# The weights' high and low parts in SBUF: slots 8200 bytes apart instead of 8192

## What is computed

```python
# block 1, per layer
x = x + 0.5 * swiglu_ffn(rmsnorm(x, ffn1_norm), ffn1_w_up, ffn1_w_down)     # d_ff 2816
x = x + mixer(rmsnorm(x, mix_norm), w_in, ...)   # q, k, v of 1536 columns, gated unit 2048, gates 2048;
                                                 # dilated attention, 31-tap convolution, projections
x = x + 0.5 * swiglu_ffn(rmsnorm(x, ffn2_norm), ffn2_w_up, ffn2_w_down)
x = rmsnorm(x, final_norm)
# block 2, per layer
p = rmsnorm_2(x, norm1) @ w_in                   # Fourier part, q, k, v
x = x + concat(norm(fourier_mix(u)), norm(windowed_gqa(q, k, v))) @ w_o
up = dwconv_centred(rmsnorm_2(x, norm2) @ w_up)  # 3 taps
x = x + (silu(gate) * val) @ w_down
```

## Time and profile before

| | |
|---|---|
| median of 3 runs | 1957.04 us (1954.49 to 1960.55) |
| profiled execution | 1957.0 us, the span as well |
| TensorE, matmuls | busy 1910.4 us (98%), 15828 |
| TensorE, weight loads | busy 1841.5 us (94%), 15828 |
| VectorE | busy 1471.9 us (75%) |
| ScalarE | busy 1104.8 us (56%) |
| GpSimd | busy 41.9 us (2%) |
| DMA | 368.57 MB, mean 188 GB/s |
| granted TensorE clock | mean 0.998 |

### The profile page before, as it was taken

How to read it: one execution, slowest core, us unless ns; L and a number is a source line. 1 busy time by engine, 2 the same in 40 slices (tenths; PEclk the granted TensorE clock), 3 DMA queues, 4 the chain that set the end, 5 groups by cost and what they waited for, 6 DMA issues and landing times.

```text
span 1957.0 us, 38879 instructions
## 1 busy us (share of the span) xinstructions
PE 1910.4 (98%) x15828; PEld 1841.5 (94%) x15828; DVE 1471.9 (75%) x2159; ACT 1104.8 (56%) x1414; POOL 41.9 (2%) x52
## 2 busy tenths in 40 slices
PE   7999999999999999999999999999999999999998
PEld 7999898799999999998988999999889999889998
DVE  6555799987765585558999877555888777878777
ACT  5444666576644464446666765444665655656554
POOL 0000011000000000000110000000000000000000
PEclk9999999999999999999999999999999999999999
DMA  6556599634555545555996446555335554435554
GB/s 251 202 178 224 190 290 272 185 99 148 208 201 185 192 172 196 183 214 183 292 279 173 107 141 217 202 184 184 130 109 196 208 193 156 141 119 192 193 193 153
DMA packets 62731, 368.57 MB, mean 188 GB/s; under 512 B 8096, under 2 KB 8352, under 8 KB 25888
## 3 DMA queue, kind: packets, MB, share of 16 engines
q1 hardware_dynamic: 54704, 339.37, 49.7%
q0 software_dynamic: 6912, 25.17, 7.2%
q10 hardware_dynamic: 1008, 2.51, 0.3%
HBM read 359.68 MB, written 1.05 MB: 184 GB/s over the span
## 4 chain that ended last, share of the span: by engine, by line
PE 74%; DVE 17%; ACT 4%; DMA 3%; issue 2%; SPq 0%; DVEq 0%; ACTq 0%
PE bank L447 23%; PE bank L448 23%; PE bank L449 22%; DVE lo L1651 5%; DVE cv L1899 4%; ACT hi L1070 1%; DVE zt L1862 1%; DMA zt<-zt 1%; DMA lo<-in_w 1%; PE bank L626 1%; PE bank L653 1%; ACT n_hi L1132 1%; PE bank L639 1%; PE bank L611 1%; DVE qk L1864 0%
## 5 line engine op out<-in xcount | busy, mean ns | idle before, releaser
L1651 DVE TENSOR_TENSOR lo<-raw,hi 128x2048 fp32r<-128x2048 f32 (+1 forms) x336 | 663.5, 1976 | 200.8 <-ACT hi L1070 200.1
L1070 ACT ACTIVATE hi<-raw 128x2048 fp32r<-128x2048 f32 (+1 forms) x336 | 598.7, 1784 | 108.8 <-PE bank L449 98.0
L447 PE MATMUL bank<-n_hi,hi 128*128 128x256 f32 x2256 | 637.9, 283 | 20.8 <-DVE lo L1926 11.5
L448 PE MATMUL bank<-n_lo,hi 128*128 128x256 f32 x2256 | 631.4, 280 | 0.0
L449 PE MATMUL bank<-n_hi,lo 128*128 128x256 f32 x2256 | 631.3, 280 | 0.0
L447 PEld LDWEIGHTS bank<-n_hi,hi 128*128 128x128 f32 x2256 | 430.8, 191 | 26.7 <-DVE lo L1926 11.5
L448 PEld LDWEIGHTS bank<-n_lo,hi 128*128 128x128 f32 x2256 | 424.9, 188 | 1.3 <-issue 1.0
L449 PEld LDWEIGHTS bank<-n_hi,lo 128*128 128x128 f32 x2256 | 425.1, 188 | 0.0
L447 PE MATMUL bank<-h_hi,hi 128*128 128x256 f32 x1152 | 330.8, 287 | 7.0 <-DVE h_lo L1655 3.9
L449 PE MATMUL bank<-h_hi,lo 128*128 128x256 f32 x1152 | 321.5, 279 | 0.0
L448 PE MATMUL bank<-h_lo,hi 128*128 128x256 f32 x1152 | 321.5, 279 | 0.0
(11 more groups left out here) (263 smaller groups left out, 2317.8 us busy)
## 6 DMA issues: line engine op xcount, KB each, us to landing
raw<-in_w SPq DMA_DIRECT2D x286, 1024.0 KB, 4.9
raw<-in_w SPq DMA_DIRECT2D x53, 512.0 KB, 4.0
lo<-in_w POOLq DMA_DIRECT2D x48, 512.0 KB, 9.1
zt<-zt SPq DMA_DIRECT2D x96, 64.0 KB, 6.9
bv<-in_bv SPq DMA_DIRECT2D x2, 768.0 KB, 6.1
spread<-in_spread SPq DMA_DIRECT2D x2, 768.0 KB, 7.9
x<-in_x ACTq DMA_DIRECT2D x4, 256.0 KB, 10.2
out_x<-sq SPq DMA_DIRECT2D x1, 1024.0 KB, 3.9
```

The lines of the kernel that those rows point to most:

```text
L447: mm(out, w_hi, a_hi, start=start, stop=False, skip_group_check=True)
L448: mm(out, w_hi, a_lo, start=False, stop=False, skip_group_check=True)
L1070: fn(hi[:, s, 0:w], raw[:, s, 0:w], ACT.Copy).then_inc(sem["hi"], 1)
L1651: v.tensor_tensor(lo[:, s, 0:w], raw[:, s, 0:w], hi[:, s, 0:w].bitcast(F32), ALU.subtract)\
```

## The change

`hi` and `lo` get 2050 elements a slot instead of 2048, of which the last two stay unused. Slot 1 so begins 8200 bytes after slot 0 and slot 2 16400 after it. Behind `hi` stand 448 further bytes, and behind `lo` 128 in the place of 192. Slot 0 of `hi` stays where it was; slot 0 of `lo` and everything behind it move up by 512 bytes and keep their place modulo 512. Modulo 512 a tile of weights begins at 128 in slot 0, 136 in slot 1 and 144 in slot 2. `raw` is not changed. The two lines that took a whole slot (1282, 1944) now name its 2048 elements. In the changed kernel a line behind 252 has a number larger by one.

```diff
--- before.py
+++ after.py
@@ -248,9 +248,10 @@
         return nc.alloc_sbuf_tensor_at(name, shape, dt, offset=at)
 
     raw = sb("raw", [P, SLOTS, CW], F32)
-    hi = sb("hi", [P, SLOTS, CW], F32R)
-    lo = sb("lo", [P, SLOTS, CW], F32R)
-    state["at"] += 192
+    hi = sb("hi", [P, SLOTS, CW + 2], F32R)
+    state["at"] += 448
+    lo = sb("lo", [P, SLOTS, CW + 2], F32R)
+    state["at"] += 128
     x = sb("x", [P, KT, S], F32)
     h_hi = sb("h_hi", [P, KT, S], F32R)
     h_lo = sb("h_lo", [P, KT, S], F32R)
@@ -1279,7 +1280,7 @@
             direct_high(2, x, gain)
             direct_high(3, x, gain)
             act.wait_ge(load[1], 16)
-            fn(hi[:, 1, :], raw[:, 1, :], ACT.Copy).then_inc(sem["hi"], 1)
+            fn(hi[:, 1, 0:CW], raw[:, 1, :], ACT.Copy).then_inc(sem["hi"], 1)
             for p in range(4):
                 fn(xsq[:, 2 * p:2 * p + 2, :], x[:, 2 * p:2 * p + 2, :], ACT.Square).then_inc(sem["sq"], 1)
             take("prm")
@@ -1941,7 +1942,7 @@
             arrived(2)
             arrived(3)
             v.wait_ge(sem["hi"], 2)
-            v.tensor_tensor(lo[:, 1, :], raw[:, 1, :], hi[:, 1, :].bitcast(F32), ALU.subtract).then_inc(sem["lo"], 1)
+            v.tensor_tensor(lo[:, 1, 0:CW], raw[:, 1, :], hi[:, 1, 0:CW].bitcast(F32), ALU.subtract).then_inc(sem["lo"], 1)
             v.wait_ge(sem["prmld"], 16)
             v.wait_ge(sem["h"], 4)
             v.tensor_copy(prm[:, 0:NP1], prm_all[:, 0:NP1]).then_inc(sem["prm"], 1)
```

## The result

The changed kernel takes **1974.75 us** in the median of 5 runs (1972.92 to 1981.69); the kernel before beside it 1957.04 us (5 runs, 1951.53 to 1966.55). The ratio is 1.0093, with a 95% interval of 1.0069 to 1.0118: slower by about 18 us, where 8.5 us less were forecast. The profiled execution has a span of 1975.5 us, and its time is 1977.33 us; so 1.8 us lie around the span, which the text ahead of the prediction took for nothing. Span against span the difference is 18.4 us.

What follows compares the result with a forecast made beforehand. The prediction took TensorE's pitch, steady at 117.6 or 113.1 ns for the same matmul, to bound the kernel. It summed 1957.0 - 10.5 (pitch drawn anew) + 2.0 (settling) = 1948.5 us, with a range of 1930 to 1974 us.

Steps and rivals of the forecast that it cites:

- What bounds the kernel: Whole kernel: TensorE, busy 98% of the span; time is matmuls times pitch, steadily 117.6 ns in block 1, 113.1 in block 2.
- Part 1: Feed-forward loops: each change of slot draws the pitch anew, 42% of matmuls long instead of 5950 of 8635, -10.5 us.
- The settling cost: Feed-forward chunk borders: a fall to the short pitch costs some 20 ns, at roughly half of 198 borders, +2.0 us.
- Part 2: TensorE's weight loads in slots 1 and 2: beginning at an odd 8 bytes takes no longer, 0 us.
- Parts 3, 4 and 5: VectorE's and ScalarE's reads and writes, accumulating DMAs into lo, and value chunks at displaced places: 0 taken for each.
- part 5: Value chunks, hi and lo as moving operand: four of six a layer displaced, at most 1.5 us either side, 0 taken.
- the long pitch takes the loops of block 2: Slower rival, feed-forward loops of block 2: they turn long too, 12.1 us more, 1969.1 us; chance 0.16.
- the third pitch in slots 1 and 2: TensorE in slots 1 and 2: the sign that a displaced load costs by itself.
- the displaced load: Slower rival, slots 1 and 2: 1 ns on 10552 matmuls, 1967.6 us; chance 0.11, shared with later accumulating transfers.
- the far end of part 2: Displaced weight loads: a whole step between the pitches, 4.5 ns, on two thirds of all matmuls (10552), +47 us.
- the rows of line 589: Existing weight loads, half 8 bytes off a multiple of 16: all 96 last 132 to 137 ns; basis for part 2's 0.
- no change: Rival: the lock hangs on restarts alone, not on 8 bytes; 1957 us, a few microseconds either side; chance 0.19.

## Why the prediction was wrong

*What bounds the kernel* held: the time is the pitch, and at the addresses of before it has two steady values that are kept until a disturbance. The runs with an extra matmul show that directly.

*Part 1* failed, and this is the step: "I take it that each such step draws the pitch anew, with the share that the restarts show." It had -10.5 us. A new setting does happen, but only in slot 0, a third of the chunks, and it is no draw with the share of the restarts: it goes by turns in block 1 and is long from the third turn on in block 2. For slots 1 and 2 I took a displacement as a push and not as another place: that the two pitches of before belong to the distance of 192 bytes, which all its matmuls share, and that 184 and 176 bytes have others and no short one, could not be seen from one distance, and I did not list it as a rival. Measured, slots 1 and 2 go from 117.7 to 118.3 and 118.7 ns in block 1, and from 113.6 and 113.5 to 118.4 and 119.9 ns in block 2. Instead of -10.5 us the four stages of block 1 gave -0.7 us and the two of block 2 +13.6 us (one execution of each kernel). The step's upper end, +12.1 us for block 2 all long, came near that by another road: there the displaced slots are past the long pitch. And the mixers, for which the step put nothing because waits draw the pitch anew there, paid 5.2 us: the displaced slots have nothing short to draw there either.

*The settling cost* of +2.0 us is too small to be told apart in this.

*Part 2*, 0 for the load itself, held in its letter: with slots 64 and 128 bytes off the kernel loses as much (1973.34 us), so no price of an odd 8 bytes is needed; for distances within 8 bytes of 192 it is not excluded. The Trainium skill's rule of 16-byte lines ("Advanced Engine Details and Errata", SBUF Cachelines), by which the prediction had slot 1 alone pay 15 us (a third of all 15828 matmuls at its 3.5 ns would be 18.5 us), is not borne out for the loaded operand: slot 2, at 16 bytes, pays as much as slot 1. For the moving operand, where 8 bytes do cost (120.0 ns), it could be the reason, which no run here separates.

*Parts 3, 4 and 5* held: VectorE's and ScalarE's splits took 1977 and 1784 ns in the mean (1976 and 1784 before), the DMAs landed no later, and the matmuls of the value chunks took 400 and 393 ns (400 and 392 before). Of the six value chunks of a layer of block 1 three are displaced, chunks 34, 35 and 58, and not four as part 5 has it; its bound was a little too wide.

*The rivals.* The slower end that came true was a mixture: "the long pitch takes the loops of block 2" in size (1969.1 us), and the third pitch in slots 1 and 2, named as the mark of the displaced load, in what the profile shows. I had taken 1 ns for it and called 4.5 ns the far end; in block 2 it was 4.8 and 6.4 ns. The range ended at 1974.0 us, and 1974.75 us lies just outside. It was cut for the far end of part 2 without a row against that end, while the rows of line 589, 64 columns wide and not pressed, had no bearing on a pitch. The rule that TensorE never waits on anyone (the Trainium skill, "SBUF — State Buffer", Who interferes with whom) gave no change. The measurement decides against using it so: TensorE's pitch for one and the same instruction runs from 113.3 to 120.0 ns with addresses alone. That its own two reads get in each other's way is my reading of this; no trace shows the reads.

## What to carry to other kernels

Where TensorE is the bound, compare the distance of the starts of one and the same matmul between stages: a difference of some per cent without a wait was an operand's address or a lock here, and a table of stretches with counts shows it. The addresses of weights and moving operand belong together; a padding that moves one of them is to be tested at the distance that it makes, not as a disturbance. And where a lock has two states, one small matmul (0.03 us here) can choose between them, but it must be seen in the trace which one it chose.

## What the runs showed that was not expected

The pitch of a 128x128 float32r matmul of 256 columns depends on the distance, modulo about 256 bytes, between its two operands: 113.3 or 117.8 ns at 192, 117.6 to 120.0 ns in the mean at the fourteen other distances tried; 4 bytes to either side (188, 196) the short one is gone. It comes back for single chunks at 320 and 448, and some other distances have two levels too: 118.7 and 120.1 ns at 176, 118.6 and 120.0 ns at 384. Displacing hi alone costs as much as displacing both, displacing lo alone nothing in the sum. A moving operand that begins 8 bytes off a multiple of 64 gives 120.0 to 120.3 ns in every slot, and 2.2% more time. And an unbroken run of matmuls at the distance of 192 stays in its pitch for 150 us and more, until a wait or something of another width or at another distance passes.
